# A decoder layer in fp32 on one core: the sample group's delta-rule recurrence rewritten so that TensorE multiplies key and query by the old states, and the new states are made in the branch stage

## The reference, cut to what matters

```python
def step(s, xs):
    q_, k_, v_, b_, g_ = xs
    s = s * jnp.exp(g_)[..., None, None]
    u = b_[..., None] * (v_ - jnp.einsum('bhd,bhde->bhe', k_, s))
    s = s + jnp.einsum('bhd,bhe->bhde', k_, u)
    return s, jnp.einsum('bhd,bhde->bhe', q_, s)
```

## Time and profile before

| | us |
|---|---|
| median of 3 runs (lowest, highest) | 1735.18 (1733.95, 1736.27) |
| the profiled execution's own time | 1736.62 |
| its span (granted clock of TensorE, mean) | 1734.8 (0.992) |
| busy: TensorE, its weight loads, VectorE, ScalarE, GpSimd | 1694.1, 1640.5, 963.0, 577.0, 486.7 |
| sample recurrence beside the last gate units, from the trace | 786 to 832.7 |
| branch stage | 832.7 to 901 |
| mix stage and first LayerNorm | 901 to about 1005 |

### The profile page before, as it was taken

One profiled execution on the slowest core, in us unless ns is written; L12 is line 12 of the kernel. 1 busy time (PEld: TensorE's weight loads), 2 busy tenths in 40 slices (PEclk: granted clock), 3 DMA queues, 4 the chain that ended last, 5 costly groups with the idle time before them and its releaser, 6 DMA issues.

```text
span 1734.8 us, 35396 instructions
## 1 busy us (share of the span) xinstructions
PE 1694.1 (98%) x14036; PEld 1640.5 (95%) x14036; DVE 963.0 (56%) x1638; ACT 577.0 (33%) x1162; POOL 486.7 (28%) x283
## 2 busy tenths in 40 slices
PE   8999999999999999999999999999999999999997
PEld 7999999999999888887999999999999999999996
DVE  2003337777456677755574679766666666311147
ACT  3124333444432554531232353222322223301124
POOL 1121111111211112211232342444554443624320
PEclk9999999999999999999999999999999999999998
DMA  4111104456552444325451032454444415522102
GB/s 184 49 44 36 41 36 108 118 179 150 165 191 90 131 138 130 109 71 197 176 216 69 25 135 86 176 186 158 152 151 157 170 73 223 204 77 82 58 31 98
DMA packets 134961, 211.13 MB, mean 122 GB/s; under 512 B 60064, under 2 KB 100160, under 8 KB 133440
## 3 DMA queue, kind: packets, MB, share of 16 engines
q1 hardware_dynamic: 134144, 208.83, 35.7%
q10 hardware_dynamic: 720, 0.93, 0.2%
HBM read 157.20 MB, written 79.94 MB: 137 GB/s over the span
## 4 chain that ended last, share of the span: by engine, by line
PE 90%; DVE 5%; issue 1%; DMA 1%; ACT 1%; SPq 1%; POOL 1%; DVEq 0%; ACTq 0%; POOLq 0%
PE U L943 33%; PE B L1426 15%; PE U L1048 11%; PE U L1426 6%; PE U L1349 4%; PE U L1492 3%; PE B L943 3%; PE B L1034 2%; PE B L1009 1%; PE B L1026 1%; PE B L1194 1%; PE B L1226 1%; DVE acc L2439 1%; PE U L1467 1%; PE B L1136 1%
## 5 line engine op out<-in xcount | busy, mean ns | idle before, releaser
L832 POOL TENSOR_TENSOR wl<-stage,wh 128x1024 fp32r<-128x1024 f32 x81 | 195.0, 2407 | 764.3 <-ACT wh L1509 751.1
L943 PE MATMUL U<-xh,wh 128*128 128x344 f32 x960 | 313.8, 327 | 0.2 <-ACT qkv L1513 0.2
L943 PE MATMUL U<-xl,wh 128*128 128x344 f32 x960 | 307.3, 320 | 0.0
L943 PE MATMUL U<-xh,wl 128*128 128x344 f32 x960 | 307.2, 320 | 0.0
L943 PEld LDWEIGHTS U<-xh,wh 128*128 128x128 f32 x960 | 181.1, 189 | 0.6 <-ACT qkv L1513 0.5
L943 PEld LDWEIGHTS U<-xh,wl 128*128 128x128 f32 x960 | 181.2, 189 | 0.0
L943 PEld LDWEIGHTS U<-xl,wh 128*128 128x128 f32 x960 | 181.0, 189 | 0.0
L1509 ACT ACTIVATE wh<-stage 128x1024 fp32r<-128x1024 f32 x77 | 81.1, 1053 | 137.7 <-PE U L943 111.4
L1048 PE MATMUL U<-xh,wh 128*128 128x344 f32 x384 | 126.1, 328 | 0.0
L1048 PE MATMUL U<-xl,wh 128*128 128x344 f32 x384 | 125.9, 328 | 0.0
L1048 PE MATMUL U<-xh,wl 128*128 128x344 f32 x384 | 125.2, 326 | 0.0
(11 more groups left out here) (443 smaller groups left out, 4482.3 us busy)
## 6 DMA issues: line engine op xcount, KB each, us to landing
stage<-in_wu SPq DMA_DIRECT2D x126, 512.0 KB, 3.7
out_shift<-in_cache SPq DMA_DIRECT2D x16, 1022.0 KB
hid_scr<-cc SPq DMA_DIRECT2D x22, 516.0 KB, 2.9
gate_scr<-gth SPq DMA_DIRECT2D x16, 516.0 KB, 3.1
gates<-gate_scr SPq DMA_DIRECT2D x8, 1032.0 KB, 5.0
dn_scr<-thb SPq DMA_DIRECT2D x12, 512.0 KB, 2.8
tok_scr<-pre SPq DMA_DIRECT2D x48, 128.0 KB, 3.9
qkv<-in_cache SPq DMA_DIRECT2D x10, 512.0 KB, 6.6
```

The costliest lines, as they stand in the source:

```text
L832: nc.gpsimd.tensor_tensor(wl[:, par, :], stage[:, par, :], wh[:, par, :].bitcast(F32), ALU.subtract).then_inc(w_lo, 1)
L943: ins = nc.tensor.matmul(dst, a[:, par, w], b[:, xk, third(j)], start=first and n == 0 and m == 0, stop=last and n == len(ks) - 1 and m == 2)
```

## The change

The recurrence uses the old states. PE multiplies each old state by query and key together, two columns a product, 32 products in one block; q.k comes from one product with ones. DVE makes u (`s64[:, 6, 0:32]`) and the outputs from these small tiles. PE turns u into rows, ACT copies them (`vrow`), SP writes them to DRAM (`v_scr`) and reads them back spread over all partitions into `v_wide`, 2 MB in the space of `xl` tiles 4 to 7. The old states are scaled by the decay on ACT, 32 instructions of 128 columns after the sample output's high part and ahead of the branch stage's first `high`. The new states are 32 `scalar_tensor_tensor` of 128 columns on DVE, 16 after the low parts of branch tile 2 and 16 after those of tile 3; SP stores them there. The quarters of `beside` are dealt out anew (12, 3, 3, 3, 4, 4 and the rest). PE waits for the sample output's low part only ahead of the first branch tile's last third. The x tiles go to `acc`, which now lies elsewhere, after branch tile 5: two, then six in one DMA, both ahead of the loads of the first two mix units. DVE's branch loop and SP's are written out. In the FFN the windows 1, 2 and 3 are written out on DVE with `weight_sums` last; at the last window SP stores the last but one hidden tile and reads the first tile of the residual later among the loads of the hidden tiles.

```diff
+        STATE_TILES = {2: (0, 1), 3: (2, 3)}
...
-            for h in range(DN_H):
-                sp.wait_ge(ds_new, 2 * h + 2)
-                sp.dma_start(O["sS"][:, h], sS[:, h]).then_inc(state_stored, 16)
+            since(sp, v_rows, 1)
+            sp.dma_start(v_scr, vrow[:]).then_inc(v_out.sem, 16)
             gate_out(U_BRANCH - 1, (U_BRANCH - 1) % 2)
+            since(sp, v_out, 16)
+            sp.dma_start(v_wide, v_scr.rearrange("(o r) c -> o (r c)", o=1).to_broadcast([P, DN_H * SAMPLES * P])).then_inc(v_spread, 16)
             for par in (0, 1):
                 sp.wait_ge(gate_stored[par], 16 * TILES)
             sp.wait_ge(of_low, TILES + 1)
@@ -733,15 +739,19 @@
             def x_of(f, n):
                 sp.dma_start(acc[:, bass.ds(f, n), :], I["xT"][:, bass.ds(f, n), :]).then_inc(acc_in, 16)
 
-            for f, par, _ in pairs(sp, 0, KT - 2):
+            for f, par, _ in peeled(0, KT - 2):
                 load(f + (U_BRANCH + 2), par)
                 sp.wait_ge(used, f * 3 + 3)
                 gates_of(f + 2, par)
-                x_of(f, 1)
+                if f in STATE_TILES:
+                    for h in STATE_TILES[f]:
+                        sp.wait_ge(ds_new, h + 1)
+                        sp.dma_start(O["sS"][:, h], sS[:, h]).then_inc(state_stored, 16)
+            x_of(0, 2)
+            sp.wait_ge(state_stored, 16 * (1 + DN_H))
+            x_of(2, 6)
             for f in range(KT - 2, KT):
...
-            hidden_out(FT - 2)
             since(sp, hid_out, 16 * PIECES[0])
-            res_in(0, 0, 1)
             for n, done in ((0, 2), (1, 4), (2, 5), (3, 7)):
                 since(sp, p_done, FINAL * PRODUCTS + done)
+                if n == 1:
+                    hidden_out(FT - 2)
+                if n == 2:
+                    res_in(0, 0, 1)
                 hidden_in(n, HID_ROWS[n][0], xf[:, slice(*HID_ROWS[n]), :])
...
-            beside.run(5)
+            beside.run(3)
             pe.wait_ge(ds_dve, 2)
-
-            def sample_out(n):
-                h, b0 = n // 2, n % 2 * 4
-                pe.wait_ge(ds_new, n + 1)
-                for i in range(4):
-                    col = h * SAMPLES + b0 + i
-                    ins = nc.tensor.matmul(B7[:, col:col + 1], sS[:, h, b0 + i, :], s64[:, 2, col:col + 1], start=True,
-                                           stop=True)
-                return ins
-
-            for n in range(8):
-                h, b0 = n // 2, n % 2 * 4
-                pe.wait_ge(ds_scaled, n + 1)
-                bank = B56[:, n % 2, :]
-                nc.tensor.matmul(bank, dcst[:, D_ONE:D_ONE + P], sdv[:, n % 2].rearrange("p i k -> p (i k)"),
-                                 start=True, stop=False)
-                for i in range(4):
-                    col = h * SAMPLES + b0 + i
-                    ins = nc.tensor.matmul(bank[:, i * P:(i + 1) * P], s64[:, 4, col:col + 1].to_broadcast([P, P]),
-                                           sS[:, h, b0 + i, :], start=False, stop=i == 3)
-                ins.then_inc(ds_prod, 1)
-                if n > 0:
-                    sample_out(n - 1)
-            beside.run(2)
-            sample_out(7).then_inc(ds_o, 1)
-            beside.run(2)
+            nc.tensor.matmul(B7[:, 64:96], dcst[:, D_ONE:D_ONE + P], s64[:, 4, 0:32], start=True, stop=True)
+            both = s64[:, 2, :].rearrange("p (x c) -> p c x", x=2)
+            for h in range(DN_H):
+                pe.wait_ge(state_in[h], 32)
+                for b in range(SAMPLES):
+                    col = h * SAMPLES + b
+                    ins = nc.tensor.matmul(B7[:, 2 * col:2 * col + 2], sS[:, h, b, :], both[:, col, :], start=True, stop=True)
+            ins.then_inc(ds_prod, 1)
+            beside.run(4)
+            since(pe, v_ready, 1)
+            nc.tensor.transpose(B56[0:32, 1, 0:P], s64[:, 6, 0:32], ident).then_inc(v_turned_out, 1)
             pe.wait_ge(ds_act, 3)
-            nc.tensor.matmul(B34[0:32, 1, 0:1], s64[:, 0, 0:32], one, start=True, stop=True).then_inc(ds_pe, 1)
-            beside.run(3)
+            nc.tensor.matmul(B7[0:32, 128:129], s64[:, 0, 0:32], one, start=True, stop=True).then_inc(ds_pe, 1)
+            beside.run(4)
             pe.wait_ge(rs_ready, 2)
-            nc.tensor.matmul(B34[:, 1, 64:96], s64[0:32, 1, 1:2].to_broadcast([32, P]), ident[0:32, 0:32], start=True,
+            nc.tensor.matmul(B7[:, 160:192], s64[0:32, 1, 1:2].to_broadcast([32, P]), ident[0:32, 0:32], start=True,
                              stop=True).then_inc(ds_pe, 1)
             beside.rest()
...
-            pe.wait_ge(of_low, TILES + 1)
             pe.wait_ge(taken, 3 * U_BRANCH)
 
             def branch(f, par, skip_wait):
@@ -1300,6 +1296,8 @@
                 for j in range(THIRDS):
                     if not skip_wait:
                         pe.wait_ge(used, f * 3 + (j - 2))
+                    elif j == 2:
+                        pe.wait_ge(of_low, TILES + 1)
...
-            nc.scalar.activation(s64[:, 0, 0:32], B7[:, 0:32], ACT.Square).then_inc(ds_act, 1)
+            nc.scalar.activation(s64[:, 0, 0:32], s64[:, 6, 32:64], ACT.Square).then_inc(ds_act, 1)
+            act.wait_ge(v_turned_out, 1)
+            nc.scalar.activation(vrow[:], B56[0:32, 1, 0:P], ACT.Copy).then_inc(v_rows.sem, 1)
             beside.rest()
             act.wait_ge(of_ready, TILES + 1)
             nc.scalar.activation(oh[:, 2:6, SEQ:TOK], sof[:], ACT.Copy).then_inc(of_high, 1)
+            act.wait_ge(ds_prod, 1)
+            for col in range(DN_H * SAMPLES):
+                state = sS[:, col // SAMPLES, col % SAMPLES, :]
+                nc.scalar.activation(state, state, ACT.Copy, scale=s64[:, 3, 32 + col:33 + col]).then_inc(ds_scaled, 1)
...
-            nc.vector.tensor_scalar(s64[:, 4, 0:32], s64[:, 2, 32:64], -1.0, None, ALU.mult)
-            nc.vector.tensor_tensor(s64[:, 4, 32:64], s64[:, 2, 32:64], s64[:, 3, 0:32], ALU.mult)
             nc.vector.tensor_scalar(s64[:, 5, 0:32], sin[:, 8:12, :].rearrange("p h b -> p (h b)"), 0.5, None, ALU.mult)
-            nc.vector.tensor_scalar(s64[:, 2, 0:32], s64[:, 2, 0:32], DN_D ** -0.5, None, ALU.mult).then_inc(ds_dve, 1)
+            st.link(nc.vector.tensor_scalar(s64[:, 2, 0:32], s64[:, 2, 0:32], DN_D ** -0.5, None, ALU.mult))
+            nc.vector.tensor_tensor(s64[:, 4, 0:32], s64[:, 2, 0:32], s64[:, 2, 32:64], ALU.mult).then_inc(ds_dve, 1)
             dve.wait_ge(ds_dve, 2)
-            across = lambda ap: ap.unsqueeze(2).to_broadcast([P, 4, P])
-
-            def group_of(n):
-                h, b0 = n // 2, n % 2 * 4
-                col = h * SAMPLES + b0
-                return sS[:, h, b0:b0 + 4, :], lambda part, base: across(s64[:, part, base + col:base + col + 4])
-
-            def decayed(n):
-
-                state, by = group_of(n)
-                dve.wait_ge(state_in[n // 2], 32)
-                st.link(nc.vector.tensor_tensor(state, state, by(3, 32), ALU.mult))
-                nc.vector.tensor_tensor(sdv[:, n % 2], same(ident), by(5, 0), ALU.mult).then_inc(ds_scaled, 1)
-
-            decayed(0)
-            for n in range(8):
-                if n < 7:
-                    decayed(n + 1)
-                state, by = group_of(n)
-                dve.wait_ge(ds_prod, n + 1)
-                st.link(nc.vector.tensor_tensor(sdv[:, n % 2], heads4(B56[:, n % 2, :]), by(4, 32), ALU.mult))
-                nc.vector.tensor_tensor(state, state, sdv[:, n % 2], ALU.add).then_inc(ds_new, 1)
-                dve.wait_ge(ds_new, n + 1)
+            dve.wait_ge(ds_prod, 1)
+            read = B7[:, 0:64].rearrange("p (c x) -> p x c", x=2)
+            strength, decay = s64[:, 3, 0:32], s64[:, 3, 32:64]
+            st.link(nc.vector.tensor_tensor(s64[:, 4, 32:64], read[:, 1, :], decay, ALU.mult))
+            st.link(nc.vector.tensor_tensor(s64[:, 7, 0:32], s64[:, 5, 0:32], s64[:, 4, 32:64], ALU.subtract))
+            nc.vector.tensor_tensor(s64[:, 6, 0:32], s64[:, 7, 0:32], strength, ALU.mult).then_inc(v_ready.sem, 1)
+            st.link(nc.vector.tensor_tensor(s64[:, 7, 32:64], read[:, 0, :], decay, ALU.mult))
+            since(dve, v_ready, 1)
+            st.link(nc.vector.tensor_tensor(s64[:, 4, 32:64], B7[:, 64:96], s64[:, 6, 0:32], ALU.mult))
+            nc.vector.tensor_tensor(s64[:, 6, 32:64], s64[:, 7, 32:64], s64[:, 4, 32:64], ALU.add).then_inc(ds_o, 1)
+            dve.wait_ge(ds_o, 1)
             dve.wait_ge(ds_pe, 4)
-            nc.vector.tensor_scalar(s64[0:32, 1, 1:2], B34[0:32, 1, 0:1], 1.0 / DN_D, RMS_EPS, ALU.mult, ALU.add).then_inc(
+            nc.vector.tensor_scalar(s64[0:32, 1, 1:2], B7[0:32, 128:129], 1.0 / DN_D, RMS_EPS, ALU.mult, ALU.add).then_inc(
                 ss_ready, 1)
             dve.wait_ge(ds_pe, 5)
-            st.link(nc.vector.tensor_copy(s64[:, 5, 32:64], B34[:, 1, 64:96]))
+            st.link(nc.vector.tensor_copy(s64[:, 5, 32:64], B7[:, 160:192]))
```

(43 more changed lines are left out.)

22 lines of the change are left out of this document (12 added, 10 removed).

## The result

The changed kernel takes 1739.56 us (median of 20 executions, 1735.94 to 1744.3), the kernel before 1736.2 (1733.95 to 1738.25): ratio 1.0021, 95% interval 1.0015 to 1.0027. A second comparison gave 1.0032 (1.0019 to 1.0044). The forecast was 3.5 us more than the 1735.18 it stood on; measured are 3.4 more than 1736.2. The profiled execution has a span of 1737.6 us against 1734.8. The sum came out right, but in part by luck, since its errors cancel: the new pauses are shorter than forecast, and the low clock costs more.

A forecast was written before the change was run, and what follows sets the result against it. TensorE, busy 98% of the span, was taken as the bound. Terms -17.0 - 0.3 + 4.5 + 7.5 + 3.7 + 5.1 = +3.5 us on 1735.18 gave 1738.7, range 1728 to 1745.

The forecast's parts named there:

- Part 1: Recurrence: 25.3 us of TensorE time removed, 8.3 added by old-state products, -17.0 us; earlier branch start, -0.3 us.
- Part 2: Branch tile 1: ScalarE's 32 scalings, 9.5 us, delay the high weights, so TensorE stands still, +4.5 us.
- Part 3: Branch stage: VectorE's new-state products, held by GpSimd, make TensorE pause twice, at tiles 4 and 5, +7.5 us.
- Rival B: Branch stage: VectorE has room for the state products, without GpSimd's hold; 7.5 + 1.7 us faster, 1729.5; chance 0.17.
- Part 4: Mix stage start: eight x tiles stand ahead of mix unit 0's load, so TensorE waits, +3.7 us.
- rival C: Mix start: x tiles don't stand in the way, DMA engines share the loads; -3.7 - 1.7 us, 1733.3; chance 0.13.
- Part 5: Clock: pauses at tile 1, tile 5 and mix start each cost half of 3.4 us at 1.2 GHz, +5.1 us.
- Rival D: Clock: each of three pauses drops it for 6.9 us, not 3.4; +5.2 us, 1743.9; chance 0.12.
- Part 6: FFN: the 3.2 us pause in window 2 moves to window 4, 0 us; bounds -4.9 to 0.
- Rival A: FFN: the pause goes, as VectorE catches up in windows 2 and 3; -4.9 us, 1733.8; chance 0.20.

The follow-up runs named there:

- memory order alone: The kernel before with the FFN's tiles and the accumulator trading places in memory, and VectorE waiting for stored gates at the branch start: 1735.71 us, ratio 0.9996.
- the run with the load ahead: The changed kernel with mix unit 0's load issued ahead of the eight x tiles and mix unit 1's behind them: 1733.08 us, 0.9979 of the kernel before.
- the spread block: The changed kernel with a gate-unit quarter behind every fourth state product in the recurrence: 1745.33 us, 1.0048 of the kernel before; again 1740.34, 1.0031.

## Why the prediction was right, and where it was wrong

The time (1738.7 forecast, 1739.56 measured), the range and the sign all held. By its own parts:

- **Part 1, -17.0 and -0.3:** the work was costed nearly rightly: with the new block's clock at 1.00 the gain is 17.9. Of that 1.7 us is the low clock of the old recurrence, which the 25.3 us hold; in the profile of "memory order alone" the old recurrence has no low clock and takes 37.56 us from the product of L1254 to the branch start, against 39.12. In the changed kernel the gain is 13.3. The step that failed is "64 x 0.118 = 7.5 us": it took the price of loads from a stretch at full clock, where products of 128 columns stood among them, for a stream that has two. The loads took 9.68 us, and the low clock lasted 10.2 us, where the old recurrence had 3.4.
- **Part 2, +4.5:** 4.1. The 32 scalings took 9.46 us (9.5).
- **Part 3, +7.5 in pauses of 2.85 and the rest:** 1.8 and 3.3, 5.1 together. From the last third of tile 2 VectorE needs 9.27 us, not 10.3: 2.69 to the products for 2.92, and 6.55 for 4.8 + 0.3 + 2.3. The products start 0.27 apart, the lower end, and the drains lie in them. The hold by GpSimd was right: 2.2 us in each tile. Rival B, which needed no hold, falls by it. One product of 2.52 us stands among those of 0.346 (median), which the forecast had at 0.35. Its fixed parts of 0.154 and 0.217 us are estimates by 1.04 ns a column: in the trace before, VectorE's additions from a bank to `acc` took 0.512 us with 344 columns (L2687, median) and 0.870 with 688 (L2439).
- **Part 4, +3.7:** 4.6. The load was seen to land 17.0 us after the issue of the last gates, where 15.8 were worked out. No run shows the 1.9 us of start that these hold beside the stream's 13.9: the 1032 KB of gates land 5.0 us after their issue, 2.5 us of it at 417 GB/s, which leaves some 2.5 by estimate. The order was the cause, as the run with the load ahead shows (rival C falls). The windows from 888 to 900 show 424, 460 and 399 GB/s, where the forecast took 417.
- **Part 5, +5.1:** 6.8 in the profile, since the pause at tile 1 had 6.8 us of low clock behind it; the block's low clock isn't in this part at all. Rival D (6.9 us behind each pause) is half right: nine profiles of the changed kernel and its variants have the 4.1 us pause at tile 1, and the clock is low there for 6.8 us in five and 3.4 in four. At the mix start, in nine profiles too, it is the same: five and four. At the 3.3 us pause of tile 5 it is 3.4 us in all eight. Half of the mean stretches, the cost by estimate, is 7.0 us for the three, where 5.1 were forecast: that term was too small, and which length comes is the execution's.
- **Part 6, 0:** the pause moved to window 4 as argued (3.0 us, at 1155.2 to 1158.1). Rival A is false. The 1.2 us of the memory order weren't foreseen: "`acc`, which now lies elsewhere" had no term.

Set against the medians: the low clock is taken to cost (1 - mean clock) x span, an estimate. The middle execution has 0.992 before (in the groups of the later comparisons; 0.991 in one) and 0.987 after: 13.9 and 22.6 us, +8.7. The rest, from the terms above, is -17.9, less the 1.7 us that the low clock of the old recurrence had in it, so -16.2, +13.8 of pauses and -1.2 of the memory order: -3.6. Together +5.1 where 3.4 were measured; the clocks are given to 0.001, which leaves 0.9 us open on either side. Counted in the same way, the forecast had -17.3 + 1.7 + 15.7 = +0.1 for the rest and +3.4 for the clock. Taken the other way round, what was measured less the clock's part leaves -5.3 for the rest, and in the second comparison (0.992 and 0.9845: +13.1 for the clock, +7.1 measured) -6.0. So by this estimate the change is slower by its clock alone; its work and its waits together are a gain of some 4 to 6 us. The waits and the clock aren't independent, though: of the low clock in the first profile 13.6 us stand at the new pauses and 10.2 in the block.

## What to carry to other kernels

When a block of TensorE is thinned out, ask what streams behind its loads: a run of products with few columns lowered the clock here as long as a pause did (6.8 or 10.2 us against 3.4 or 6.8), and 128 columns behind a load took no longer than two (64 loads: 7.23 us with 128; at full clock 38 records of products with two and 37 with 128 in the same 4 us). Work that is moved off a saved stretch needs a place where its engine idles and nothing waits for what stands behind it in its queue; here all three pauses came from the place and none from the work, since with the same work in other places they were gone. A moved wait is looked for where the order of the work changes next.

## What the runs showed of the hardware

- The clock fell with TensorE busy 4.00 of 4.00 us, in the block of two-column products, in both profiles of the changed kernel and in five of its variants. The busy time in the profile's page didn't tell the two cases apart: the same 64 loads at the same busy time kept 1.00 with 128 columns.
- The spread between executions of one kernel is the clock's: the changed kernel took 1735.94 us at a mean clock of 0.989 and 1744.3 at 0.984, and the stretches of low clock in its profiles are 3.4, 6.8 or 10.2 us long, but for the last 20 us of the span; the 17 us of the spread block are the longest elsewhere. The kernel before ranges alike, from 1730.09 us at 0.995 to 1740.07 at 0.989. Single profiles therefore differ by several us for the same code: compare waits and durations between them, and the clock over many runs.
- The place of tiles in memory changed the length of an FFN window by 0.4% (20.165 and 20.09 us); which tile and why is open.
